# Moving the experts' up-weight loads from SyncE's queue to ScalarE's

## The chip, the cores and the metric

The kernel runs on one core of a Trainium2 chip. The metric is the device time of one execution in microseconds (us). The core has a matrix engine (TensorE, PE in the profile), VectorE (DVE), ScalarE (ACT), GpSimd (POOL) and SyncE (SP), and 16 DMA engines that all of these feed through queues.

## The reference

One layer of a hybrid trunk on 384 tokens (256 latent, 128 context) of width 1024: adaptive layer norm, attention and gated linear attention in parallel, an output projection, and then a mixture of experts. The change lies in the last part:

```
w, e_idx = top-1 of 4 groups, then top-2 of 8 experts in it
for e in range(32):
    hid = silu(t @ exp_w_gate[e]) * (t @ exp_w_up[e])      # 1024 -> 256
    y = y + comb[:, e:e+1] * (hid @ exp_w_down[e])         # 256 -> 1024
```

Everything is float32. Each expert has three weight matrices of 1 MB (1.049 million bytes): gate, up and down, 96 MB in all.

## The kernel before

Each engine has its own program; semaphores join them. The mixture of experts runs over the 32 experts in order, each with up to 64 token rows gathered by GpSimd (two halves of a row on two sets of partitions). There are six weight buffers (`NBUF` = 6). Expert n uses buffer n % 6, so its weights can be loaded when expert n-6 has used its own.

TensorE's program for expert n is: gate-and-up matmuls of expert n+1 (`next_gate_up`, L1742, 32 instructions); transpose of expert n's hidden values (L1773); transposes of the gathered tokens of expert n+2 (`next_tokens`, L1728); down matmuls of expert n (`next_down`, L1751, 8 instructions). The gate-and-up matmuls wait for 32 counts on `ew_in` of their buffer (16 each for gate and up), and for ScalarE's copy of the tokens. At experts 28 to 31 extra matmuls (`residual`, L1783) are placed between; the first of them waits for a small matrix that VectorE makes at expert 28 (L1183).

ScalarE's program for expert n is: wait for `gu_full` (the gate-and-up matmuls of n are done), silu (L1394), copy of the tokens of expert n+1 (`tokens`, L1376). VectorE multiplies silu by up (L1134), copies the transposed hidden values (L1138), forms the row gains (L1143, L1144) and evicts the down result (L1152). After expert 29 VectorE also waits for a small row of token numbers that SyncE loads (L608), and builds a selection matrix from it (L1192), ahead of expert 30's copy.

SyncE issues the weights. Those of experts 0 to 4 and most of 5 are issued ahead of the expert loop. Then, for n from 6 on: wait until the gate-and-up matmuls of expert n-6 are done, issue gate n and up n (`load_gate_up`, L455); wait until the down matmuls of expert n-7 are done, issue down n-1 (`load_down`, L469, or L465 for the buffer in two parts). Behind the last down come the token row (L608), and the loads and stores of the end.

A page's L455 is the `dma_start` in `load_part`, for gate and up alike.

Of the kernel before, what the change touches and what calls it, by code (L numbers as in the profile page):

```python
# [25 lines left out]
GROUPS, EPG, NE, DE = 4, 8, 32, 256  # L26
# [198 lines left out]
def program(nc, T):  # L225
    ctx = ExitStack()
    with ctx:
# [3 lines left out]
        def sem(name):  # L231
            return ctx.enter_context(nc.semaphore(name))
# [119 lines left out]
        NBUF = len(ebuf)  # L352
# [82 lines left out]
        ew_in = [sem(f"ew_in{j}") for j in range(len(ebuf))]  # L435
# [17 lines left out]
        def load_part(eng, name, g, e, s, landed):  # L453
            src = T[name][0].rearrange("e (p k) n -> p e k n", k=KT)
            eng.dma_start(ebuf[s][0][g], pick(src, e)).then_inc(landed, 16)  # L455

        def load_gate_up(eng, e, s, landed):

            for g, name in enumerate(("exp_w_gate", "exp_w_up")):
                load_part(eng, name, g, e, s, landed)  # L460

        def load_down(eng, e, s, landed):
            if s == PARTED:
                for h in range(2):
                    eng.dma_start(ebuf[s][1][h], T["exp_w_down"][0, e, h * P:(h + 1) * P, :]).then_inc(landed, 16)  # L465
                return
            both_halves = whole[s][:, 2 * KD:3 * KD].rearrange("p (h n) -> p h n", h=2)
            src = T["exp_w_down"][0].rearrange("e (h p) n -> p e h n", p=P)
            eng.dma_start(both_halves, pick(src, e)).then_inc(landed, 16)  # L469
# [5 lines left out]
        def pick(src, e):  # L475
            a = src[:, e:e + 1] if isinstance(e, int) else src[:, bass.ds(e, 1)]
            names = "a b c d"[0:2 * (len(a.shape) - 2) - 1]
            return a.rearrange(f"p e {names} -> p (e {names.split()[0]}) {' '.join(names.split()[1:])}")
# [7 lines left out]
        def overflow(eng, again):  # L486

            eng.wait_ge(S["rank_ready"], 1)
            most = eng.value_load(maxu[0:1, 0:1], min_val=0, max_val=TOKENS)
            with eng.If(most > SLOT_ROWS):  # L490
                with eng.Fori(1, ROUNDS) as r:
                    with eng.If(r * SLOT_ROWS < most):
                        again(r)
# [3 lines left out]
        def _(sp):  # L497
# [89 lines left out]
            for n in range(NBUF, NE + 1):  # L587
                if n < NE:
                    sp.wait_ge(S["gu_full"], n - NBUF + 1)
                    load_gate_up(sp, n, n % NBUF, ew_in[n % NBUF])  # L590
                m = n - 1
                if m >= NBUF:
                    sp.wait_ge(S["y_full"], m - NBUF + 1)
                load_down(sp, m, m % NBUF, ed_in[m % NBUF])
# [622 lines left out]
        def _(act):  # L1217
# [157 lines left out]
            def tokens(b, done):  # L1375
                A_(xTe[:, b].rearrange("p k n -> p (k n)"), banks[0][:, :], ACT.Copy).then_inc(done, 1)  # L1376
# [13 lines left out]
            for n in range(NE):  # L1390
                act.wait_ge(S["gu_full"], n + 1)
                if n:
                    act.wait_ge(S["hid_ready"], n)
                A_(sg, gub[n % 2][:, 0:P], ACT.Silu).then_inc(S["silu_ready"], 1)  # L1394
                if n + 1 < NE:
                    act.wait_ge(S["xTe_full"], n + 2)
                    tokens((n + 1) % 2, S["xTe_ready"])
                if n == CHECK:
                    overflow(act, experts)
# [491 lines left out]
```

## Time and profile before

| | |
|---|---|
| median of 3 runs | 699.74 us (697.8 to 699.88) |
| profiled execution | 700.73 us, span 699.0 us |
| mean granted TensorE clock | 0.976 |
| PE busy | 629.5 us (90%) |
| DVE, ACT, POOL busy | 284.6, 108.5, 111.9 us |
| DMA queue of SyncE (q1) | 143.60 MB |
| DMA queue of ScalarE (q10) | 24.21 MB |
| DMA queue of GpSimd (q0) | 8.28 MB |

Times in the rows are in us from the start of the span, unless marked ns. A row of the timeline gives the start, the duration, the engine and line, the operation, the tile written and read, and the number of instructions merged; in brackets stands the idle time of the engine ahead of it and what ended it. SPq and ACTq are the DMA instructions of SyncE and ScalarE: their duration is that of the issue, not of the transfer.

### The profile page before, as it was taken

The numbers are of one execution on the slowest core, as the hardware profiler recorded it, in microseconds if no ns is written. First come the engines' busy times: TensorE is split into PE (matmuls) and PEld (weight loads), VectorE is DVE, ScalarE is ACT, GpSimd is POOL, SyncE is SP. The second block draws the span as 40 slices with busy tenths as digits, with TensorE's granted clock in tenths as the row PEclk, the third lists the DMA queues.
The fourth block names the chain that finished last, engine by engine and source line by source line (L and its number), as shares of the span: only waits on it lengthen the run. The fifth ranks groups of instructions, "written<-read, shape, count | busy, mean of one in ns | idle before, by whom it ended". The sixth has DMA issues, their size and how long they took to land.

```text
span 699.0 us, 8281 instructions
## 1 busy us (share of the span) xinstructions
PE 629.5 (90%) x3245; PEld 332.3 (48%) x3245; DVE 284.6 (41%) x606; ACT 108.5 (16%) x227; POOL 111.9 (16%) x113
## 2 busy tenths in 40 slices
PE   2699999999999999999999999899999778788984
PEld 0284344564344445454444456666665444444531
DVE  1421443226756456233223786133333223322247
ACT  0020252220011121125010011211111111111100
POOL 3000000020310000000000221443334222331100
PEclk9879999999999999999999999999999999999998
DMA  9987463336430321408969059699999999999852
GB/s 335 368 264 251 135 228 122 120 120 240 142 125 0 120 81 41 120 0 258 370 274 360 31 225 375 224 412 413 410 413 413 412 413 410 413 413 414 336 213 90
DMA packets 59336, 176.63 MB, mean 253 GB/s; under 512 B 10453, under 2 KB 12533, under 8 KB 51105
## 3 DMA queue, kind: packets, MB, share of 16 engines
q1 hardware_dynamic: 42672, 143.60, 53.5%
q10 hardware_dynamic: 10880, 24.21, 9.7%
q0 software_dynamic: 5744, 8.28, 3.4%
q8 instruction: 27, 0.44, 0.3%
q14 instruction: 13, 0.10, 0.0%
HBM read 174.58 MB, written 11.96 MB: 267 GB/s over the span
## 4 chain that ended last, share of the span: by engine, by line
PE 67%; DMA 14%; SPq 9%; DVE 6%; issue 2%; ACT 1%; POOL 1%; ACTq 0%; DVEq 0%; POOLq 0%
PE bank L1477 24%; DMA X<-exp_w_up 10%; PE bank L1742 10%; PE bank L1649 6%; PE bank L1663 6%; SPq L455 4%; PE bank L1751 4%; DMA X<-w_ada 3%; PE bank L1429 2%; SPq L465 2%; PE bank L1608 2%; SPq L469 1%; PE bank L1530 1%; PE bank L1669 1%; PE bank L1627 1%
## 5 line engine op out<-in xcount | busy, mean ns | idle before, releaser
L1477 PE MATMUL bank<-W,Y 128*128 128x512 f32 (+1 forms) x432 | 182.6, 576 | 0.0
L1477 PEld LDWEIGHTS bank<-W,Y 128*128 128x128 f32 x432 | 80.0, 190 | 86.7 <-issue 84.1
L1742 PE MATMUL bank<-X,Y 128*64 128x256 f32 x704 | 83.9, 392 | 15.9 <-DMA X<-exp_w_up 14.7
L1742 PEld LDWEIGHTS bank<-X,Y 128*64 128x64 f32 x704 | 54.8, 141 | 50.9 <-DMA X<-exp_w_up 23.9
L636 POOL TENSOR_TENSOR rstd<-ss,cst 128x1 f32<-128x1 f32 (+3 forms) x21 | 22.5, 1073 | 335.6 <-DVE ss L767 335.6
L1138 DVE COPY abias<-bank 128x128 f32<-128x128 f32 x32 | 9.3, 291 | 119.9 <-PE bank L1773 119.9
L679 POOL DMA_INDIRECT Y<-h_rows,gidx x32 | 41.3, 1290 | 94.1 <-PE bank L1728 88.9
L1751 PE MATMUL bank<-X,abias 128*64 128x512 f32 x176 | 42.6, 602 | 1.9 <-issue 1.9
L684 POOL DMA_INDIRECT pair_rows<-PTr,sidx x32 | 32.4, 1012 | 65.6 <-DVE PTr L1152 59.1
L1649 PE MATMUL bank<-W,Y 128*128 128x512 f32 x96 | 42.0, 594 | 0.3 <-PE bank L1649 0.3
L1742 PE MATMUL bank<-W,Y 128*64 128x256 f32 (+1 forms) x320 | 36.0, 340 | 6.7 <-DMA Y<-exp_w_up 4.2
L1663 PE MATMUL bank<-X,Y 128*128 128x512 f32 x96 | 41.6, 593 | 0.4 <-PE bank L1649 0.4
L1394 ACT ACTIVATE abias<-bank 128x128 f32<-128x128 f32 x32 | 8.9, 277 | 184.5 <-PE bank L1742 184.5
L1152 DVE TENSOR_TENSOR PTr<-bank,abias 128x512 f32<-128x512 f32 x32 | 22.1, 692 | 26.4 <-PE bank L1751 26.4
L1742 PEld LDWEIGHTS bank<-W,Y 128*64 128x64 f32 x320 | 23.4, 142 | 18.8 <-DMA Y<-exp_w_up 5.9
L1663 PEld LDWEIGHTS bank<-X,Y 128*128 128x128 f32 x96 | 18.1, 190 | 23.2 <-issue 23.2
L998 DVE COPY PTr<-bank 128x384 f32<-128x384 f32 (+1 forms) x24 | 10.2, 464 | 46.0 <-PE bank L1615 45.9
L1649 PEld LDWEIGHTS bank<-W,Y 128*128 128x128 f32 x96 | 17.9, 190 | 22.3 <-issue 22.3
L834 DVE TENSOR_TENSOR PTr<-bank,abias 128x512 f32<-128x512 f32 x12 | 8.3, 692 | 49.0 <-PE bank L1429 27.6
L1144 DVE SCALAR_TENSOR_TENSOR abias<-PTr,wc,abias 128x512 f32<-128x512 f32 x32 | 24.0, 752 | 1.1
L1257 ACT ACTIVATE X<-bank 128x512 f32<-128x512 f32 (+1 forms) x15 | 8.4, 560 | 98.0 <-PE bank L1477 98.0
L1376 ACT ACTIVATE Y<-bank 128x512 f32<-128x512 f32 x32 | 19.1, 597 | 23.5 <-PE bank L1728 23.5
(225 smaller groups left out, 700.1 us busy)
## 6 DMA issues: line engine op xcount, KB each, us to landing
X<-exp_w_gate SPq DMA_DIRECT2D x22, 1024.0 KB
X<-exp_w_up SPq DMA_DIRECT2D x22, 1024.0 KB
X<-exp_w_down SPq DMA_DIRECT2D x22, 1024.0 KB
W<-w_in SPq DMA_DIRECT2D x8, 2048.0 KB, 8.5
Y<-w_ada ACTq DMA_DIRECT2D x8, 2048.0 KB, 9.4
W<-exp_w_gate SPq DMA_DIRECT2D x10, 1024.0 KB
W<-exp_w_up SPq DMA_DIRECT2D x5, 1024.0 KB
W<-exp_w_down SPq DMA_DIRECT2D x5, 1024.0 KB
```

The source lines that it names most:

```text
L455: eng.dma_start(ebuf[s][0][g], pick(src, e)).then_inc(landed, 16)
L636: nc.gpsimd.tensor_tensor(rstd[:, 0:n], ss[:, 0:n], const("mhalf", 0, n), ALU.pow)\
L679: pool.indirect_dma_start(G[:, n % NSLOT, :], None, h2_d, bass.IndirectOffsetOnAxis(ap=gidx[:, n:n + 1], axis=0), bounds_check=2 * TOKENS ...
L684: pool.indirect_dma_start(yp_d, bass.IndirectOffsetOnAxis(ap=sidx[:, n:n + 1], axis=0), Yo[:, n % NY, :], None, bounds_check=2 * TOPK * TO ...
L1144: step(V.scalar_tensor_tensor(gw, g2r[:, 1, :], wc[:, n:n + 1], gw, ALU.mult, ALU.add))
L1152: V.tensor_tensor(Yo[:, n % NY, :], banks[6][:, :], gw, ALU.mult).then_inc(S["y_ready"], 1)
L1376: A_(xTe[:, b].rearrange("p k n -> p (k n)"), banks[0][:, :], ACT.Copy).then_inc(done, 1)
L1477: ins = mm(bank[:, 0:cols], hT[:, i, k, :], w[:, k, :], start=k == 0, stop=k == KT - 1)
L1649: ins = mm(bank[:, :], src[:, i, k, :], w[:, m, k, :], start=k == 0, stop=k == 3)
L1663: ins = mm(bank[:, :], mT[:, i, k, :], w[:, k, :], start=k == 0, stop=k == KT - 1)
L1742: ins = mm(bank[hh * 64:hh * 64 + 64, a:b], x_[:, c, h * 64:h * 64 + 64], rhs(hh), start=k == 0 and a == 0, stop=k == KT - 1, skip_group_c ...
L1751: ins = mm(banks[6][o * 64:o * 64 + 64, :], hT_[:, hh * 64:hh * 64 + 64], wd[hh][:, o * HALF:(o + 1) * HALF], start=hh == 0, stop=hh == 1, ...
```

## The change

ScalarE issues the up weights of experts 6 to 31, each behind the silu of the expert that used the buffer before. SyncE keeps gate and down.

```diff
@@ SyncE
             for n in range(NBUF, NE + 1):
                 if n < NE:
                     sp.wait_ge(S["gu_full"], n - NBUF + 1)
-                    load_gate_up(sp, n, n % NBUF, ew_in[n % NBUF])
+                    load_part(sp, "exp_w_gate", 0, n, n % NBUF, ew_in[n % NBUF])
                 m = n - 1
                 if m >= NBUF:
                     sp.wait_ge(S["y_full"], m - NBUF + 1)
@@ ScalarE
                 if n:
                     act.wait_ge(S["hid_ready"], n)
                 A_(sg, gub[n % 2][:, 0:P], ACT.Silu).then_inc(S["silu_ready"], 1)
+                if n + NBUF < NE:
+                    load_part(act, "exp_w_up", 1, n + NBUF, n % NBUF, ew_in[n % NBUF])
                 if n + 1 < NE:
                     act.wait_ge(S["xTe_full"], n + 2)
                     tokens((n + 1) % 2, S["xTe_ready"])
```

## Rows read from the trace of the kernel before

**Rows 1.** Page, the span in 40 slices: GB/s moved by DMA.

```profile
GB/s 335 368 264 251 135 228 122 120 120 240 142 125 0 120 81 41 120 0 258 370 274 360 31 225 375 224 412 413 410 413 413 412 413 410 413 413 414 336 213 90
```

**Rows 2.** Chain of work, 440 to 699 us: start, duration, what.

```profile
639.07 23.89 DMA X<-exp_w_up
663.00 3.67 PE bank L1742 x32
```

**Rows 3.** Windows: stretch, length, busy time of each engine, clock, DMA share, GB/s.

```profile
540.00:560.00 20.00, 15.28 (x150) 9.74 (x146) 4.66 (x10) 1.75 (x4) 5.19 (x5) 1.00 1.02 415
560.00:580.00 20.00, 16.27 (x103) 8.51 (x101) 5.88 (x14) 2.62 (x6) 4.78 (x5) 0.91 1.02 412
```

**Rows 4.** Timeline of PE: starts of experts 13, 14, 17, 25, 27 to 30.

```profile
519.43 3.64 PE L1742 MATMUL bank<-X,Y 128*64 128x256 f32 x32
...
525.51 3.64 PE L1742 MATMUL bank<-X,Y 128*64 128x256 f32 x32
...
548.01 0.44 PE L1742 MATMUL bank<-W,Y 128*64 128x128 f32 x4 [2.33 <-DMA Y<-exp_w_up]
...
614.34 5.33 PE L1742 MATMUL bank<-X,Y 128*64 128x256 f32 x32 [2.22 <-DMA X<-exp_w_up]
...
631.17 5.36 PE L1742 MATMUL bank<-W,Y 128*64 128x256 f32 x32 [2.29 <-DMA W<-exp_w_up]
...
639.39 3.67 PE L1742 MATMUL bank<-X,Y 128*64 128x256 f32 x32 [0.23 <-DMA X<-exp_w_up]
...
648.28 0.44 PE L1742 MATMUL bank<-W,Y 128*64 128x128 f32 x4
...
655.30 3.62 PE L1742 MATMUL bank<-X,Y 128*64 128x256 f32 x32
```

**Rows 5.** Timeline of SyncE's queue.

```profile
445.39 0.33 SPq L455 DMA_DIRECT2D X<-exp_w_gate  x1
...
561.91 6.72 SPq L455 DMA_DIRECT2D X<-exp_w_up  x1
...
580.70 2.51 SPq L455 DMA_DIRECT2D X<-exp_w_up  x1
...
639.07 2.18 SPq L455 DMA_DIRECT2D X<-exp_w_up  x1
```

**Rows 6.** Timeline, 568 to 570 us, expert 19: ScalarE and PE.

```profile
568.57 0.28 ACT L1394 ACTIVATE abias<-bank 128x128 f32<-128x128 f32 x1 [6.78 <-PE bank L1742]
...
569.22 1.94 PE L1751 MATMUL bank<-X,abias 128*64 128x512 f32 x8
...
569.30 0.60 ACT L1376 ACTIVATE Y<-bank 128x512 f32<-128x512 f32 x1 [0.46 <-PE bank L1728]
```

**Rows 7.** Timeline, 666 to 670 us, experts 30 and 31.

```profile
666.61 0.33 PE L1773 MATMUL bank<-cst,abias 128*128 128x128 f32 x1
...
668.61 0.75 DVE L1192 TENSOR_SCALAR X<-X,gf 128x384 f32<-128x384 f32 x2 [5.43 <-DMA X<-consts]
...
669.27 0.28 DVE L1138 COPY abias<-bank 128x128 f32<-128x128 f32 x1
```

**Rows 8.** Timeline of both queues, 366 to 370 us; time to landing of L1361.

```profile
366.82 0.85 ACTq L1358 DMA_DIRECT2D Y<-x_sample  x2
...
368.17 0.53 ACTq L1361 DMA_DIRECT2D Y<-ln_b  x1
...
DMA to landing us min/median/max: 7.2/10.5/13.8
```

**Rows 9.** Windows with both queues at work.

```profile
370.00:376.00 6.00, 6.00 (x16) 2.65 (x15) 1.50 (x3) 0.00 (x0) 0.00 (x0) 1.00 1.01 420
376.00:382.00 6.00, 6.00 (x22) 3.08 (x21) 1.27 (x2) 0.36 (x1) 0.00 (x0) 1.00 1.02 388
```

**Rows 10.** Timeline of both queues from 324 us.

```profile
324.79 12.89 SPq L455 DMA_DIRECT2D X<-exp_w_gate  x1
...
325.05 0.94 ACTq L1342 DMA_DIRECT2D X<-modulation_rows  x2
```

## The prediction

> **What bounds the kernel now.** I read the page's slices first: from 454 us on (slice 27) eleven slices stand at 410 to 414 GB/s, and the rate falls only in the last three [rows 1]. The stretch of the experts, from 440 us to the end, is therefore the one that matters. The chain of work there follows one up transfer after another: the last one, expert 31's, is issued at 639.07 and TensorE starts on it at 663.00 [rows 2]. The windows show the same: between 540 and 560 DMA is full and PE has 15.28 us of work in 20 [rows 3].
>
> The starts of the experts' gate-and-up matmuls (L1742) tell where PE is limited by what. Experts 13 and 14 start 6.08 us apart (519.43, 525.51): that is PE's own pace. Experts 17 and 27 start at 548.01 and 631.17, so 8.32 us each, and there each waits for its up weights; from 27 to 31 it is 7.96 us each [rows 2, 4]. Of these, 3 x 1.049 MB at 413 GB/s are 7.62 us; the other 0.34 to 0.70 us are the gathered and scattered rows. So weights set the pace from expert 16 on, and PE has about 2 us to spare in each expert.
>
> Two more things matter. SyncE is far behind the buffers: its queue is full and an issue takes 2.5 us or even 6.7 us [rows 5]. Expert 31's up could have gone when expert 25's matmuls were done (614.34 + 5.33 = 619.7), but it went at 639.07 [rows 4, 5]. And the last expert steps hang on the small load of the token row (L608), last in that same queue: VectorE waits for it until 668.61 and copies expert 30's transposed hidden values only at 669.27, though PE had them at 666.94 [rows 7].
>
> **The change, part by part.** No byte is added or taken away: 26 up transfers of 1.049 MB move from SyncE's queue to ScalarE's.
>
> *ScalarE's issues.* In the trace its queue takes 0.53 us for a 512 KB load, and 0.94 for two [rows 8, 10]. I take 0.45 us. The place is behind the silu: silu at 568.57 to 568.85, then ScalarE stands idle until the tokens' copy at 569.30 [rows 6]. The issue fills just this hole. Even if it pushed the copy by 1.2 us, PE would not see it, as it is in the down matmuls until 569.22 + 1.94 = 571.16 and the copy is done at 569.90. Cost 0. For the first expert, where this cover is smaller, it is at most 0.5 us, far ahead of the place where PE begins to wait for weights. The up also goes later than gate, by the silu (0.28) and the issue; the gate transfer, 2.5 us at full rate, is then still running. Cost 0.
>
> *SyncE.* It loses 26 issues of 2.5 us or so, all of them waits in a full queue. Nothing else gains by this: the total of bytes ahead of the token row stays. Worth 0.
>
> *The order in which bytes are served.* This is the part that counts. Before, everything stood in one line: gate n, up n, down n-1. Now ups stand in a line of their own, which is short, beside a long one. When two queues have work, both are served: four loads of 512 KB on ScalarE's queue, issued from 366.82 to 368.17 beside 4.2 MB on SyncE's, landed by 368.17 + 13.8 = 382.0, that is 2.1 MB out of some 5.5 MB moved (4.85 of it from 370 to 382), a share of 0.38 [rows 8, 9]. There ScalarE's rows were 4 KB against 8 KB; up rows are as long as gate rows and longer than down's, so I take a half. An up needs a third of the traffic to keep up, so ups will run ahead of gates until only the buffers hold them. When PE waits for gate n, expert n-1's matmuls are done and up n+5 has been issued: the lead is up to 5 ups, 5 x 1.049 / 0.413 = 12.7 us of traffic that before came after gate n.
>
> The Trainium skill (DMA: Bandwidth & Descriptors, section "Queues, rings and completion order") has each engine go round the queues that have work, packet by packet; the rows above agree with turns of this kind, and no run yet shows the size of a turn.
>
> *What the lead costs.* In the middle nothing: PE starts to wait at about expert 12 or 13 instead of 16 and falls up to 12 us behind, but five gates and five downs (10.5 MB) stay queued, DMA never rests, and the last byte lands when it did. At the end it does cost. When up 31 has landed, the rest are pairs of gate and down: 2.097 MB / 413 GB/s = 5.08 us, with rows 5.4 to 5.8 us, say 5.6. This is faster than PE's 6.08 us. So traffic that PE could have overlapped with its work comes too late for it. Gate 31 lands where up 31 did, at 663.0, since behind it stand only down 30, down 31 and the token row as before. Back from there: gate 26 at 663.0 - 5 x 5.6 = 635.0. From here PE goes at its own pace: expert 27 at 641.1, 28 at 647.2; from 28 to 29 it takes 8.9 us as before (639.39 to 648.28; a matmul waits for VectorE there), so 29 at 656.1; then 7.0 us each (648.28 to 655.30), so 30 at 663.1 and 31 at 670.1 instead of 663.0 [rows 2, 4].
>
> *What of this reaches the end.* PE transposes expert 30's hidden values 3.61 us after expert 31's start (666.61 - 663.00), so at 673.7, and VectorE's copy can follow when the transpose is done (0.33), at 674.1, instead of 669.27 [rows 2, 7]. The wait for the token row, which hid the first part, is gone. The sum is 0 + 0 + 0 + (674.1 - 669.27) = +4.8 us. Behind this point stands the same chain as before.
>
> The profiled execution took 700.73 us (span 699.0), 1.0 above the median of 699.74; the sum is a difference, so it goes on the median: 704.5 us.
>
> *Bounds.* With pairs at 5.8 us gate 26 lands at 634.0: +3.8; at 5.4 us, 636.0: +5.8. Some experts ran their matmuls at the slower clock after waiting (5.36 us instead of 3.67, expert 27) [rows 4]; if that meets expert 26, where PE has no spare time any more, it adds 1.7, up to +7.5. With a lead of three ups gate 27 lands at 638.0 and gate 28 at 646.2, which gives +3.8; with two, only +1.2 (gates 28 and 29 at 643.6 and 651.8, experts 29, 30, 31 at 652.5, 659.5, 666.5); with one, 0. So the forecast needs a lead of three. Its own range is 702.5 to 707.5.
>
> **Rivals.**
> *A: the lead stays under three, no change.* The chip could serve the queues so that ups get little more than their third, or nearly in the order of issue. Then gates land as before, 699.7 us. For it: the total is the same, and all of the stretch is full. Against it: the share of 0.38 with the shorter rows. The Trainium skill (DMA: Bandwidth & Descriptors, "Rules for kernel authors") says that spreading DMAs over issuing engines does not help bandwidth; by that rule alone the time would be this one.
>
> *B: two queues carry more, faster.* In 370 to 376 us, with both queues at work, the rate was 420 GB/s against 412 to 415 [rows 3, 9]. Over the 223 us from gate 6's issue (445.4) to 668.6 each per cent is 2.2 us [rows 5, 7]. 420 would give 1.7%, 3.8 us: 696.0 without the lead, 700.7 with it. With the lead it must be over 426 GB/s (3.1%, 6.9 us) to come out faster by 0.3%, which no row shows.
>
> *C: ScalarE is held up in its issue, slower still.* SyncE's queue is full, and ScalarE's issue might wait for SyncE's to end: 2.5 us often, 6.7 at times [rows 5]. Tokens' copies then come late; most of it vanishes in PE's 2 us, but the last ones, at experts 24 and 25, could shift PE by up to 6.7 - 1.3 - 2 = 3.4 us: 708. Against it: SyncE sat in one issue from 324.79 to 337.68, and within this ScalarE issued two loads in 0.94 us [rows 10]. The Trainium skill (Perfetto Trace Analysis, "DMA Instruction — HWDGE (DVE, Sync)") says that the descriptor generator is locked for one user at a time; that would speak for C, and the row speaks against a lock that lasts as long as the stall.
>
> *D: the mix is slower.* From 376 to 382 the rate was 388 [rows 9]; the rows there were partly short. At 400, 3.2% less, the end comes 7.1 us later: 711.6.
>
> **How the numbers follow.** Forecast 0.54, A 0.25, B 0.10, C 0.06, D 0.05. A measurement of this kernel can tell about 0.3%, 2.1 us: the bounds are 697.6 and 701.8. Slower: 0.52 of the forecast, C and D: 0.63. Same: A, and 0.02 of the forecast's low end: 0.27. Faster: B, 0.10. The range leaves out most of B, D and the top of C: 698.5 to 708.5.
>
> **What the new profile would show.** ScalarE's queue with 26 up issues of 0.3 to 0.5 us, and 27.3 MB more in its queue (24.2 before). Copies of tokens that end before the down matmuls do. PE's waits named after gate instead of up. First waits at expert 12 or 13. Expert 26 at 634 to 636, then no wait for DMA; expert 31 at 669 to 671; the token row still in by about 668.6. I am wrong if expert 31 starts before 665 (A: ups do not lead; B: the rate is above 420 from 460 to 640), or if an issue on ScalarE lasts longer than 2 us (C).

## The result and the profile after

The changed kernel takes 704.72 us (median of 8 runs, 703.31 to 706.78) against 699.81 us (8 runs, 697.8 to 703.01): ratio 1.0067, 95% interval 1.0041 to 1.0093, so 4.9 us slower between the medians. The forecast was 704.5. Only executions that ran undisturbed are compared; one of the 12 of the kernel with ups 12 to 31 four experts later took 2218 us and is left out of its ratio.

The profiled execution took 703.31 us, its span is 701.5. It reached the experts' loop 3.04 us earlier than the one of before: gate 6 is issued at 442.35 against 445.39 [rows 5]. Such a shift comes with every execution (in the runs below this issue stands between 441.6 and 445.0, whatever was changed behind it), so the two traces are compared by distances from that issue.

The page, parts 2 and 3 (slices, and queues with packets, MB, share of the engines):

```profile
GB/s 334 368 265 266 157 187 153 88 120 240 144 121 0 120 119 3 120 1 312 376 243 326 31 284 335 309 414 413 412 412 413 413 413 412 414 412 406 240 188 90
...
q1 hardware_dynamic: 38928, 116.33, 44.1%
q10 hardware_dynamic: 14624, 51.47, 19.0%
```

The rate in the full slices is what it was, 412 to 414 in ten of the eleven and 406 in the last, against 410 to 414 [rows 1]. 27.3 MB have gone from SyncE's queue to ScalarE's. What the two queues then do is in part 6 (KB each, median us from issue to landing):

```profile
X<-exp_w_gate SPq DMA_DIRECT2D x22, 1024.0 KB, 28.6
X<-exp_w_down SPq DMA_DIRECT2D x22, 1024.0 KB, 29.6
X<-exp_w_up ACTq DMA_DIRECT2D x18, 1024.0 KB, 9.5
```

An up now lands 9.5 us after its issue, a gate 28.6: this is the lead. For expert 31 the two issues and their times to landing are:

```profile
625.77 0.34 ACTq L455 DMA_DIRECT2D X<-exp_w_up  x1
X<-exp_w_up ACTq DMA_DIRECT2D x1, 1024.0 KB, 9.1
...
638.90 2.21 SPq L455 DMA_DIRECT2D X<-exp_w_gate  x1
X<-exp_w_gate SPq DMA_DIRECT2D x1, 1024.0 KB, 21.0
```

The last up lands at 634.9 us, the last gate at 659.9. Read in the same way, gates 27 to 31 land at 638.6, 643.9, 649.2, 654.6 and 659.9: one pair of gate and down every 5.3 us. Waits from 440 us on (engine, tile and line, what ended the wait: us in total, times, longest):

```profile
PE bank L1744 <- DMA X<-exp_w_gate: 13.2, 10, 2.1
...
PE bank L1753 <- DMA X<-exp_w_down: 10.8, 11, 1.8
...
PE bank L1744 <- DMA W<-exp_w_gate: 4.7, 5, 1.2
```

PE waits for gates, as expected (17.9 us with the rows of both tiles), and also for downs (12.0 us with two smaller rows), which the prediction did not name. The timeline of PE (L1742 of before is L1744 here) gives the starts of experts 12 and 25 to 31 (29 is the row of 0.44 us):

```profile
514.80 3.93 PE L1744 MATMUL bank<-X,Y 128*64 128x256 f32 x32 [0.32 <-DMA X<-exp_w_up]
...
622.05 3.67 PE L1744 MATMUL bank<-X,Y 128*64 128x256 f32 x32 [1.03 <-DMA X<-exp_w_gate]
...
630.27 3.67 PE L1744 MATMUL bank<-X,Y 128*64 128x256 f32 x32 [1.18 <-DMA X<-exp_w_gate]
...
638.57 3.67 PE L1744 MATMUL bank<-W,Y 128*64 128x256 f32 x32 [0.88 <-DMA W<-exp_w_gate]
...
644.69 3.64 PE L1744 MATMUL bank<-X,Y 128*64 128x256 f32 x32
...
653.54 0.44 PE L1744 MATMUL bank<-W,Y 128*64 128x128 f32 x4
...
660.55 3.62 PE L1744 MATMUL bank<-X,Y 128*64 128x256 f32 x32
...
667.48 3.62 PE L1744 MATMUL bank<-X,Y 128*64 128x256 f32 x32
```

The first row names up, but it is the gate that came last there. Gate and up count on one semaphore, and where the gate's issue ends first (experts 6 to 12) the view takes the first landing for the gate's. ScalarE's queue settles it: it carries nothing but ups here, and from 442.3 to 470 us it moved 4.25 MB, four ups, while by the view only two would have landed.

```profile
q10 hardware_dynamic: 583, 4.25, 37.1%
```

The reader should see where the brackets end: from expert 28 on no wait for a transfer is left in them and PE goes at its own pace, 6.1, 8.9, 7.0 and 6.9 us from one start to the next. Gate 28 landed 0.8 us ahead of its matmuls, gate 31 already 7.6 us ahead. In before the transfers fed it until expert 31 [rows 2, 4]. Expert 31 starts 667.48 - 442.35 = 225.1 us after gate 6's issue; in before it was 663.00 - 445.39 = 217.6 [rows 2, 5]. That is 7.5 us later. The tail behind it:

```profile
667.75 0.69 DVE L1152 TENSOR_TENSOR PTr<-bank,abias 128x512 f32<-128x512 f32 x1 [1.61 <-PE bank L1753]
668.36 0.74 DVE L1192 TENSOR_SCALAR X<-X,gf 128x384 f32<-128x384 f32 x2
...
671.39 0.29 DVE L1138 COPY abias<-bank 128x128 f32<-128x128 f32 x1 [2.30 <-PE bank L1775]
```

VectorE no longer waits for the token row (it had 5.43 us of that [rows 7]) but for PE. From expert 31's start to the end of the span it is 701.5 - 667.48 = 34.0 us, against 699.0 - 663.00 = 36.0. So 7.5 - 2.0 = 5.5 us between the two profiled executions, and 4.9 between the medians.

That ScalarE's issue costs nothing can be read off its own rows:

```profile
568.64 0.28 ACT L1394 ACTIVATE abias<-bank 128x128 f32<-128x128 f32 x1 [8.16 <-PE bank L1744]
568.64 0.33 ACTq L455 DMA_DIRECT2D X<-exp_w_up  x1
568.69 0.65 PE L1730 MATMUL bank<-cst,Y 128*128 128x128 f32 x4
569.37 0.60 ACT L1376 ACTIVATE Y<-bank 128x512 f32<-128x512 f32 x1 [0.46 <-PE bank L1730]
569.40 1.94 PE L1753 MATMUL bank<-Y,abias 128*64 128x512 f32 x8
```

The tokens' copy waits 0.46 us for PE's transposes, exactly as without the issue [rows 6], and is done at 569.97, 1.37 us before the down matmuls end. The issues at expert 0, and at two experts while SyncE is in its longest issue:

```profile
442.35 0.28 ACT L1394 ACTIVATE abias<-bank 128x128 f32<-128x128 f32 x1 [2.56 <-PE bank L1744]
442.36 0.35 ACTq L455 DMA_DIRECT2D X<-exp_w_up  x1
...
500.48 13.50 SPq L455 DMA_DIRECT2D W<-exp_w_gate  x1
...
502.71 0.33 ACTq L455 DMA_DIRECT2D X<-exp_w_up  x1
...
508.83 0.33 ACTq L455 DMA_DIRECT2D Y<-exp_w_up  x1
```

The up goes 0.01 us after its silu's start, beside it; all 26 issues take 0.33 to 0.36 us; and twice it goes while SyncE is stuck in an issue of 13.50 us.

### The profile page after: what moved, and what is told of

Same layout as the page of the kernel before. It is cut to its first block, busy times and chain, and to the rows that moved or that the text cites. A ratio compares the mean times of both kernels' runs of the same rounds, so it can differ in the third digit from the quotient of the medians.

```text
span 701.5 us, 8281 instructions
## 1 busy us (share of the span) xinstructions
PE 624.4 (89%) x3245; PEld 325.1 (46%) x3245; DVE 284.6 (41%) x606; ACT 108.8 (16%) x227; POOL 112.1 (16%) x113
## 4 chain that ended last, share of the span: by engine, by line
PE 64%; DMA 22%; DVE 8%; SPq 3%; issue 2%; ACT 1%; POOL 1%; DVEq 0%; ACTq 0%; POOLq 0%
PE bank L1479 24%; DMA X<-exp_w_gate 10%; DMA W<-exp_w_gate 9%; PE bank L1744 8%; PE bank L1651 6%; PE bank L1665 6%; PE bank L1753 4%; DMA X<-w_ada 3%; PE bank L1431 2%; PE bank L1610 2%; PE bank L1532 1%; SPq L465 1%; PE bank L1730 1%; PE bank L1629 1%; SPq L556 1%
## 5 line engine op out<-in xcount | busy, mean ns | idle before, releaser
L1744 PE MATMUL bank<-X,Y 128*64 128x256 f32 x704 | 80.8, 382 | 14.3 <-DMA X<-exp_w_gate 13.2
L1744 PEld LDWEIGHTS bank<-X,Y 128*64 128x64 f32 x704 | 52.1, 137 | 49.9 <-DMA X<-exp_w_gate 22.0
L1744 PE MATMUL bank<-W,Y 128*64 128x256 f32 (+1 forms) x320 | 34.3, 328 | 4.7 <-DMA W<-exp_w_gate 4.7
L1744 PEld LDWEIGHTS bank<-W,Y 128*64 128x64 f32 x320 | 22.2, 137 | 16.5 <-DMA W<-exp_w_gate 9.1
L1651 PEld LDWEIGHTS bank<-W,Y 128*128 128x128 f32 x96 | 17.9, 190 | 22.3 <-issue 22.3
L1753 PEld LDWEIGHTS bank<-X,abias 128*64 128x64 f32 x176 | 11.3, 137 | 28.7 <-issue 14.9
## 6 DMA issues: line engine op xcount, KB each, us to landing
X<-exp_w_gate SPq DMA_DIRECT2D x22, 1024.0 KB, 28.6
X<-exp_w_down SPq DMA_DIRECT2D x22, 1024.0 KB, 29.6
```

The lines of the kernel that those rows point to most:

```text
L1651: ins = mm(bank[:, :], src[:, i, k, :], w[:, m, k, :], start=k == 0, stop=k == 3)
L1744: ins = mm(bank[hh * 64:hh * 64 + 64, a:b], x_[:, c, h * 64:h * 64 + 64], rhs(hh), start=k == 0 and a == 0, stop=k == KT - 1, skip_group_c ...
L1753: ins = mm(banks[6][o * 64:o * 64 + 64, :], hT_[:, hh * 64:hh * 64 + 64], wd[hh][:, o * HALF:(o + 1) * HALF], start=hh == 0, stop=hh == 1, ...
```

## The experiments

Theory: the ups lead, the last experts are therefore fed in pairs of gate and down, faster than PE works, and PE's own pace sets the end. Rivals: each issue on ScalarE costs; two queues move bytes at another rate. Each new kernel has 12 executions, the one with ups 26 to 31 alone 6. The ratio is not the quotient of the two medians and differs from it by up to 0.0012; a number of us given for a ratio below is 700 us times its distance from 1. The fifth and sixth columns are from each run's own trace: the distance from gate 6's issue to expert 31's start, and from there to the end of the span.

| run | median us | before, beside it | ratio (95%) | gate 6 to expert 31 | rest |
|---|---|---|---|---|---|
| before (profiled) | | | | 217.6 | 36.0 |
| the change | 704.72 | 699.81 | 1.0067 (1.0041 to 1.0093) | 225.1 | 34.0 |
| ups 6 to 25 only | 699.09 | 700.03 | 0.9993 (0.9974 to 1.0012) | 218.2 | 37.7 |
| ups 26 to 31 only | 705.28 | 700.03 | 1.0083 (1.0054 to 1.0111) | 225.1 | 34.0 |
| ups 26 to 31, two experts later | 702.67 | 700.33 | 1.0042 (1.0017 to 1.0066) | 222.9 | 34.0 |
| ups 26 to 31, four experts later | 700.47 | 700.33 | 1.0013 (0.9988 to 1.0038) | 217.7 | 37.9 |
| ups 12 to 31, four experts later | 700.25 | 700.33 | 0.9989 (0.9960 to 1.0017) | 217.9 | 36.1 |
| small stores instead | 701.93 | 700.03 | 1.0035 (1.0015 to 1.0056) | 221.6 | 36.0 |
| small copies instead | 700.00 | 700.33 | 1.0010 (0.9984 to 1.0035) | 217.9 | 36.0 |
| token row on ScalarE | 699.18 | 700.03 | 0.9986 (0.9965 to 1.0008) | 219.0 | 34.1 |
| the same again | 699.59 | 701.40 | 0.9986 (0.9964 to 1.0009) | 218.4 | 34.1 |
| the change and token row | 705.32 | 701.40 | 1.0064 (1.0039 to 1.0089) | 224.9 | 34.0 |
| ups 12 to 31 later, token row | 700.07 | 701.40 | 0.9981 (0.9961 to 1.0001) | 217.9 | 34.0 |

**One part of the change alone: the first twenty ups.**

```diff
-                    load_gate_up(sp, n, n % NBUF, ew_in[n % NBUF])
+                    load_part(sp, "exp_w_gate", 0, n, n % NBUF, ew_in[n % NBUF])
+                    if n >= 26:
+                        load_part(sp, "exp_w_up", 1, n, n % NBUF, ew_in[n % NBUF])
@@ ScalarE, behind the silu
+                u = n + NBUF
+                if NBUF <= u < 26:
+                    load_part(act, "exp_w_up", 1, u, u % NBUF, ew_in[u % NBUF])
```

> Ups 6 to 25 come from ScalarE, ups 26 to 31 stand again between gate and down in SyncE's queue. Theory (the lead of the ups leaves gate-and-down pairs at the end, faster than PE works): the lead is paid back before expert 26 and the last six experts get three transfers each as before, so 0 us against before (within 1.5), with expert 31's matmuls starting 8.0 us after expert 30's landed-bound neighbours as before. Rival (ScalarE pays for each issue): 20 of 26 issues are left, so +3.8 us. Rival (two queues move bytes at another rate): 20/26 of the loss too, +3.8 us.

Measured: 0.9993. Twenty of the 26 moved transfers are free. PE's starts in the trace of this run:

```profile
622.37 3.67 PE L1747 MATMUL bank<-X,Y 128*64 128x256 f32 x32 [0.30 <-DMA X<-exp_w_up]
631.26 5.36 PE L1747 MATMUL bank<-W,Y 128*64 128x256 f32 x32 [2.60 <-DMA W<-exp_w_up]
639.46 3.67 PE L1747 MATMUL bank<-X,Y 128*64 128x256 f32 x32 [0.21 <-DMA X<-exp_w_up]
...
663.04 3.67 PE L1747 MATMUL bank<-X,Y 128*64 128x256 f32 x32 [0.58 <-DMA X<-exp_w_up]
```

These stand within 0.1 us of the rows of before (631.17, 639.39, 663.00 [rows 2, 4]), and 0.6 us later counted from gate 6's issue, waits for up and all: the lead was paid back. Both rivals asked for +3.8 us and fall.

**The other part: the last six.** The same edit with `n < 26` for SyncE and `26 <= u < NE` for ScalarE.

> Only ups 26 to 31 come from ScalarE, each behind the silu of experts 20 to 25. Theory: these six go ahead of gates 21 to 26, the last five experts are fed in pairs, and the whole loss is there: +4.9 us (3.5 to 6). Rival (cost per issue) and rival (rate of two queues): 6 of 26, so +1.1 us.

Measured: 1.0083, +5.8 us (+5.3 between the medians): the whole loss, and no less than the change (225.1 us to expert 31 in both). Six issues make it. Its last starts:

```profile
630.94 3.67 PE L1747 MATMUL bank<-X,Y 128*64 128x256 f32 x32 [0.41 <-DMA X<-exp_w_gate]
639.92 3.67 PE L1747 MATMUL bank<-W,Y 128*64 128x256 f32 x32 [0.93 <-DMA W<-exp_w_gate]
646.04 3.64 PE L1747 MATMUL bank<-X,Y 128*64 128x256 f32 x32
...
661.90 3.62 PE L1747 MATMUL bank<-X,Y 128*64 128x256 f32 x32
668.82 3.62 PE L1747 MATMUL bank<-X,Y 128*64 128x256 f32 x32
```

Again no wait for a transfer from expert 28 on, as in the change.

**Less of the lead: the same six, issued later.** Each up behind the silu two experts later than its buffer comes free (`u = n + NBUF - 2`), and four later (`- 4`).

> Ups 26 to 31 from ScalarE, but each behind the silu two experts later (22 to 27), so that PE waiting for gate n finds at most ups to n+3 served. Theory (the loss grows with the number of ups that lead): a lead of three, +3.8 us by the arithmetic of the forecast, in any case between 2.5 and 4.5 and below the run with a lead of five. Rival (moving the last six costs the same wherever they are issued): +5.3 us as with the lead of five.

> As before it, but each up behind the silu four experts later (24 to 29), so a lead of one. Theory: gates land as in before, 0 us (within 1.5). Rival (the last six on another queue cost as such): +5.3 us. A third outcome, above 1.5, would mean that up itself comes too late for its own expert; then PE's waits would be named after up.

Measured: 1.0042 (+2.9 us; +2.3 between the medians) and 1.0013 (+0.9; +0.1 between the medians; not to be told from 0). With 1.0083 for the full lead the loss falls with the lead: 7.5, 5.3 and 0.1 us in the distance to expert 31's start (225.1, 222.9 and 217.7 less 217.6). In the run with two experts less of lead PE's last wait for a weight has moved on from expert 27 to the down of expert 27, behind the start of expert 28. The same six transfers on the same queue cost nothing that these runs can tell when their lead is down to one.

**Two queues without a lead, all the way.** Ups 12 to 31 with `u = n + NBUF - 4`, ups 6 to 11 on SyncE.

> Ups 12 to 31, twenty of them, from ScalarE, each behind the silu of the expert two ahead of its own (a lead of one all the way); ups 6 to 11 from SyncE. The issues on ScalarE and the two queues are those of the change, only the lead is gone. Theory: 0 us (within 1.5). Rivals (an issue on ScalarE costs; two queues move bytes slower): 20/26 of 4.9, +3.8 us.

Measured: 0.9989. Twenty issues on ScalarE and two queues side by side cost nothing. Together with the first run this rules out both rivals.

**A suspected cost doubled: ScalarE's time behind the silu.**

```diff
                 A_(sg, gub[n % 2][:, 0:P], ACT.Silu).then_inc(S["silu_ready"], 1)
+                if n + NBUF < NE:
+                    for h in range(2):
+                        act.dma_start(scr_d[4 * n + 2 * h:4 * n + 2 * h + 2, :], cst[0:2, 0:HALF]).then_inc(S["small_out"], 16)
```

> All loads as before; behind the silu of each of the experts 0 to 25 ScalarE issues two stores of 4 KB to a scratch buffer, 0.24 us each, which takes ScalarE's queue longer (0.48 us) than one up issue (0.34) and moves 0.2 MB in all. Theory: 0 us against before. Rival (ScalarE's issue delays the tokens' copy and through it PE): +4.9 us or more.

Measured: 1.0035, +2.5 us (+1.9 between the medians), which I had not expected. The rows around one pair of stores show no delay on ScalarE:

```profile
568.02 0.28 ACT L1395 ACTIVATE abias<-bank 128x128 f32<-128x128 f32 x1 [5.17 <-PE bank L1747]
568.03 0.54 ACTq L1398 DMA_DIRECT2D scratch_rows<-cst  x2
568.75 0.60 ACT L1377 ACTIVATE Y<-bank 128x512 f32<-128x512 f32 x1 [0.45 <-PE bank L1733]
```

The copy comes when PE's transposes are done, as before [rows 6]. What grew is the traffic: from gate 6's issue at 442.45 to the end of VectorE's wait for the token row at 669.65 it is 227.2 us, against 223.2 in before. Why this one traced execution shows 4.0 us, more than the medians, stays open. So the same question was asked without transfers, with small copies (`A_(conde[:, h, :], cond[:, h, :], ACT.Copy)`, twice) at the same place:

> All loads as before; behind the silu of experts 0 to 25 ScalarE runs two small copies (128x8) on tiles nobody reads, some 0.4 us, longer than an up issue (0.33), with no transfer. It asks again what the small stores asked, without their traffic. Theory: 0 us (within 1.5), the small stores' +1.9 us being their transfers. Rival (ScalarE's time behind the silu reaches PE): +1.9 us or more here too.

Measured: 1.0010. ScalarE's time there is free. By elimination what the stores cost belongs to their transfers. The Trainium skill (DMA: Bandwidth & Descriptors, "Why a DMA increments its semaphore by 16 and not by 1") has a transfer of two rows run on two of the 16 DMA engines. That would make those two the last to finish their share; no run here shows which engines were late.

**The other place, the token row.** Its load moves from SyncE's queue to ScalarE's, at expert 28.

```diff
@@ SyncE
-            sp.wait_ge(S["slots_done"], 1)
-            sp.wait_ge(S["y_full"], CHECK)
-            sp.dma_start(tokr, T["consts"][:, NCONST:]).then_inc(S["tok_in"], 16)
@@ ScalarE
                 if n == CHECK:
                     overflow(act, experts)
+                    act.wait_ge(S["slots_done"], 1)
+                    act.wait_ge(S["y_full"], CHECK)
+                    act.dma_start(tokr, T["consts"][:, NCONST:]).then_inc(S["tok_in"], 16)
```

> All weights as before; only the token row (192 KB, last in SyncE's queue before) is issued by ScalarE at expert 28. It should land within 3 us instead of 23. Theory (behind expert 30 the end hangs on the token row, which stands last in the line): VectorE's copy for expert 30 follows PE's transpose at once, 2.1 to 2.3 us earlier, so -2.1 us. Rival (the end hangs on down 30 and down 31, which land just ahead of the token row): 0 to -0.7 us.

> The kernel with only the token row on ScalarE's queue once more, since its first interval (0.9965 to 1.0008) leaves open whether it is faster. By its trace the tail from expert 31's start is 34.05 us against 36.0: theory -1.9 us (ratio 0.9973). Rival: the gain is taken back by later waits, 0 us.

Measured: 0.9986 twice, about -1 us, with intervals that reach just over 1. The trace shows the step itself:

```profile
660.37 0.74 DVE L1189 TENSOR_SCALAR X<-X,gf 128x384 f32<-128x384 f32 x2
660.75 3.67 PE L1742 MATMUL bank<-X,Y 128*64 128x256 f32 x32 [1.10 <-DMA X<-exp_w_up]
...
664.72 0.29 DVE L1135 COPY abias<-bank 128x128 f32<-128x128 f32 x1 [3.62 <-PE bank L1773]
```

The copy of expert 30 follows expert 31's start by 3.97 us instead of 6.27, and the rest of the span is 34.1 us instead of 36.0, in both traces. The row landed 7.5 and 7.4 us after its issue, not within the expected 3, and that was early enough. But expert 31 starts 1.4 and 0.8 us later than in before (219.0 and 218.4 against 217.6): part of the 1.9 us is given back there, which leaves 0.5 and 1.1 us and fits the medians. That the row's 192 KB, now ahead of the last weights, do this is likely, not shown: the kernels without it scatter from 217.7 to 218.2.

With the change, and with the ups in small lead:

> The change, and with it the token row issued by ScalarE at expert 28. In the change the row lands at 665.45, ahead of VectorE's turn, so nobody waits for it. Theory: nothing is won by it here, +4.9 us against before as the change alone (3.5 to 6). Rival (the early row is worth 2 us wherever it is done): +2.9 us.

> Ups 12 to 31 from ScalarE with a lead of one, and the token row on ScalarE's queue. Theory: no loss from the ups, the gain of the early token row in the tail: -2 us, as for the token row alone. Rival (PE's start on expert 31 comes later with any lead): 0 us.

Measured: 1.0064 and 0.9981 (0.9961 to 1.0001). The early row wins nothing in the change, where it was never late: this shows that the 2.0 us by which the change's tail is shorter are this same wait, which the change no longer has. The last kernel has the lowest ratio of all, with an interval that just touches 1; it is not told apart from the token row alone.

Two of the kernels without a lead have a tail of 37.7 and 37.9 us in the table. Their traces say why. The last matmuls of the run with the first twenty ups, and PE's window there (length, busy times, granted clock last but two):

```profile
669.71 3.63 PE L1756 MATMUL bank<-X,abias 128*64 128x512 f32 x8 [1.87 <-issue]
```

```profile
670.00:676.00 6.00, 6.00 (x19) 1.52 (x15) 2.98 (x6) 0.00 (x0) 0.00 (x0) 0.74 0.99 356
```

PE stood idle for 1.87 us while VectorE finished its wait for the token row and its copy, and then the granted clock was 0.74 over these 6 us, 0.53 over the eight matmuls themselves, which is the lower level of 1.2 GHz: expert 30's down matmuls took 3.63 us instead of the 1.94 they take elsewhere. In before and in three other runs PE was idle there as long (1.86 to 2.05 us) and the same matmuls took 1.94 us. The wait for the token row thus costs 2.0 us, or 3.7 where the clock falls with it. Where PE is late anyway (the change, and each kernel with a lead of three or more) neither shows.

## Why the prediction was right

*The cost on ScalarE, taken as 0.* Right, by the filler run and the run of twenty ups with a lead of one. The issue even stands beside the silu, not behind it: the first up went 0.01 us after the first gate.

*SyncE's shorter work, worth 0.* Right: gate 31 goes 196.6 us after gate 6 (638.90 - 442.35), against 192.4 in before (637.82 - 445.39), and the token row lands where it did.

*The rate of the bytes.* Right. From gate 6's issue to the token row's landing (issued at 651.05, 14.4 us to land, so 665.45) it is 223.1 us, against 223.2 before.

*The lead.* Right in kind. The prediction gave up to five ups, gate 26 at 635.0 and PE free of waits from there. Counted from gate 6's issue and put on the scale of before (3.04 us added), expert 26 started at 633.3, and PE still waited 0.88 us at expert 27. So four pairs, not five, came behind PE's last wait. The prediction took a half of the traffic for the ups, by which the last one would have landed some 5 us after its issue, at 630.9 (an estimate, from 1.049 MB at half of 413 GB/s), just as expert 26 began at 630.27. It took 9.1 us and landed at 634.9; no run separates how much of this is share and how much a transfer's own delay. Between 454 and 490 us ScalarE's queue moved 6.23 of 14.87 MB, 0.42 of the traffic, and from 520 to 636 us, where the buffers held the ups back, 14.68 of 47.86, 0.31.

*PE's own pace to the end.* On that scale experts 27 to 31 started at 641.6, 647.7, 656.6, 663.6 and 670.5, against a forecast of 641.1, 647.2, 656.1, 663.1 and 670.1. That these agree within 0.5 us is in part luck. The pairs came every 5.3 us where the prediction had 5.6, which alone would have put expert 27 at 642.6; four pairs instead of five took most of that back (662.9 for gate 31 on this scale, less 4 x 5.3, is 641.7). Gate 31's own landing, forecast 663.0, was right.

*What reaches the end.* The copy of expert 30 stands at 674.4 on that scale, forecast 674.1; from before's 669.27 that is +5.2 us, forecast +4.8. The medians give 4.9. The slower clock, which could have added 1.7 us, met none of the experts from 26 on.

*The dose.* The arithmetic for a lead of three gave +3.8; the run with ups two experts later gave +2.9 (1.2 to 4.6 by its interval). For a lead of one it gave 0, measured +0.9 and -0.8 with intervals over 0.

*What it missed.* PE's waits for downs, 12.0 us in total: a down stands in the same long line as the gates (29.6 us to land). They lie in the stretch that the traffic sets, and cost nothing at the end. The first wait for a gate came at expert 12, as said, but the first for any weight was just ahead of it, 1.81 us for the down of expert 10 at 511.34.

## What to carry to other kernels

Where the DMA engines were full, the second queue gave no bandwidth; it changed who was served first. A load that overtakes others there makes those others late, and near the end of a stretch this shifts work behind the last byte: what counts is how much of the compute is left when the last bytes land. If a second queue is wanted, hold its issues back so that they do not lead. Its short line can serve a small load that stands last in the long one; here that took 1.9 us off the tail, of which the medians show about 1, not to be told from 0.

## What the runs showed of the hardware

- ScalarE can issue a DMA beside its own activation: silu at 442.35, issue at 442.36.
- A full queue of SyncE does not hold up ScalarE's: two issues of 0.33 us fell into one of 13.50 us.
- In two of the profiled runs an idle 1.9 to 2.0 us of PE near the end was followed by a granted clock of 0.53 and 1.7 us more for the next eight matmuls; in before and three other runs the same idle time was not.
- Two queues that both have 1 MB transfers waiting are both served, the shorter one far sooner (9.5 us to land against 28.6), at the same total rate. While an up was issued every 6.1 us (454 to 490 us) the shorter one moved 0.42 of the traffic.
- 52 stores of 4 KB (0.2 MB) beside a full stream of loads lengthened the stream by 4.0 us in the profiled run and the kernel by 1.9 us between the medians; their bytes alone would be 0.5 us at 413 GB/s.
